# The r and value projections of a time-mix stage as three passes of the rounded format

## What is computed

```python
x_prev = jnp.pad(x, ((0, 0), (1, 0), (0, 0)))[:, :T]
xx = x_prev - x
xs = x[None] + xx[None] * mu[:, None, None, :]
rkv = jnp.einsum('nbtd,nde->nbte', xs[:3], w_rkv)
r, k, v = rkv[0], rkv[1], rkv[2]
w_log = -jax.nn.softplus(-(w0 + jnp.tanh(xw @ w1) @ w2)) - 0.5
a = jax.nn.sigmoid(a0 + (xa @ a1) @ a2)
```

## Time and profile before

| what | value |
|---|---|
| median of 3 runs | 1343.47 us (1342.68 to 1344.71) |
| the profiled execution | 1345.18 us, its span 1343.2 us |
| mean granted clock of PE | 0.997 |
| PE busy | 1310.0 us, 98% of the span |
| DVE, ACT, POOL busy | 936.9, 655.5, 104.6 us |

### The profile page before, as it was taken

The page is one execution under the profiler, slowest core; times in us unless marked ns, Lnnn a source line. Parts: engine busy times, 40 slices in busy tenths (PEclk is TensorE's granted clock), DMA queues, the critical chain, the costliest instruction groups (busy, mean ns, idle before and its releaser), DMA issues.

```text
span 1343.2 us, 23639 instructions
## 1 busy us (share of the span) xinstructions
PE 1310.0 (98%) x9400; PEld 1130.5 (84%) x9400; DVE 936.9 (70%) x1637; ACT 655.5 (49%) x1008; POOL 104.6 (8%) x106
## 2 busy tenths in 40 slices
PE   7999999999999999999999998999999999999999
PEld 7887987888888988888888886888888888888887
DVE  6972456877777765877777697766666786676664
ACT  4532224644445685544445577543434568544431
POOL 0004062000000020000001020000001042000000
PEclk9999999999999999999999999999999999999999
DMA  9532113655543233555551550975531431573610
GB/s 309 162 126 84 47 66 122 224 188 187 187 160 111 93 126 123 201 189 188 188 186 63 188 189 1 340 271 190 186 135 54 165 122 67 220 282 141 235 63 32
DMA packets 113320, 208.51 MB, mean 155 GB/s; under 512 B 3920, under 2 KB 57552, under 8 KB 112720
## 3 DMA queue, kind: packets, MB, share of 16 engines
q1 hardware_dynamic: 113232, 207.28, 44.8%
HBM read 206.21 MB, written 1.05 MB: 154 GB/s over the span
## 4 chain that ended last, share of the span: by engine, by line
PE 87%; DVE 5%; ACT 5%; DMA 1%; issue 1%; POOL 0%; SPq 0%; ACTq 0%; DVEq 0%; POOLq 0%
PE ps L1047 21%; PE ps L994 19%; PE ps L899 11%; PE ps L999 10%; PE ps L1120 2%; PE ps L1089 2%; PE ps L1204 2%; PE ps L1469 2%; PE ps L1377 1%; PE ps L970 1%; ACT Ah L1915 1%; DVE Al L2721 1%; PE ps L1513 1%; DMA ringA<-in_w_k 1%; PE ps L1527 1%
## 5 line engine op out<-in xcount | busy, mean ns | idle before, releaser
L994 PE MATMUL ps<-hTx,Ah 128*128 128x512 f32 x1088 | 270.7, 391 | 0.0
L2728 DVE TENSOR_TENSOR Al<-ringA,Ah 128x2048 fp32r<-128x2048 f32 x74 | 169.3, 2288 | 97.2 <-ACT Ah L1925 97.2
L994 PEld LDWEIGHTS ps<-hTx,Ah 128*128 128x128 f32 x1088 | 199.7, 188 | 38.5
L999 PEld LDWEIGHTS ps<-hTx,Al 128*128 128x128 f32 x1152 | 156.7, 190 | 10.6
L1960 ACT COPY xn<-ps 128x512 f32<-128x512 f32 x72 | 42.3, 587 | 244.1 <-PE ps L999 236.8
L999 PE MATMUL ps<-hTx,Al 128*128 128x256 f32 x1152 | 160.7, 282 | 0.0
L1925 ACT CAST Ah<-ringA 128x2048 fp32r<-128x2048 f32 x76 | 145.7, 1916 | 13.1 <-PE ps L899 10.3
L1934 ACT CAST Bh<-ringB 128x1024 fp32r<-128x1024 f32 (+1 forms) x76 | 107.1, 1410 | 89.5 <-PE ps L1047 89.5
L899 PE MATMUL ps<-Ah,hTx 128*128 128x512 f32 (+1 forms) x576 | 136.6, 388 | 2.8 <-ACT Ah L1915 1.4
L2735 DVE TENSOR_TENSOR Bl<-ringB,Bh 128x1024 fp32r<-128x1024 f32 (+1 forms) x76 | 127.0, 1670 | 10.6 <-ACT Bh L1934 10.2
L1047 PE MATMUL ps<-Bh,hidh 128*128 128x512 f32 x416 | 129.9, 392 | 1.1 <-issue 1.1
(11 more groups left out here) (449 smaller groups left out, 2053.8 us busy)
## 6 DMA issues: line engine op xcount, KB each, us to landing
ringA<-in_ffn_w_in SPq DMA_DIRECT2D x44, 1024.0 KB, 7.5
ringA<-in_mlp_w SPq DMA_DIRECT2D x32, 1024.0 KB, 7.6
ringB<-in_mlp_w SPq DMA_DIRECT2D x32, 1024.0 KB, 6.9
ringB<-in_ffn_w_out SPq DMA_DIRECT2D x44, 512.0 KB, 4.2
ringA<-in_diff_w_in SPq DMA_DIRECT2D x12, 1024.0 KB, 6.3
ringA<-in_dsa_w_in SPq DMA_DIRECT2D x8, 1024.0 KB, 6.2
ringA<-in_w_r SPq DMA_DIRECT2D x4, 1024.0 KB, 8.1
ringA<-in_w_v SPq DMA_DIRECT2D x4, 1024.0 KB, 7.0
```

Of the source, the lines that this page charges most:

```text
L994: mm(o.rearrange("p (i t) -> p i t", i=2), w_hi, hTx[:, :, k * T:(k + 1) * T], start=(k == 0), stop=False)
L999: last = mm(o[:, T:2 * T], Al[:, half, k * T + j * P:k * T + j * P + P], hTh[:, k, :], start=False, stop=(k == KT - 1))
L2728: V.tensor_tensor(a_split(w, Al, half), a_half(w, (a_at[w] + par) % 2, half), a_split(w, Ah, half).bitcast(F32), ALU.subtract).then_inc(al ...
```

## The change

The r and value projections are done in the rounded format too. Each r job becomes 48 matmuls of 128x256 (two halves, three passes, eight steps). Each value job takes a whole 128-token tile and 512 columns: 24 matmuls of 128x512. ACT casts the four r weight quarters, the four value weight halves and the two inputs; the low parts of all of the r side and of value halves 0, 2 and 3 are made by POOL, those of the value input and of value half 1 by DVE. Low parts of weights are written over the weights in `ringA`. The rounded copies lie in buffers that are free at the time. Since some of them lie where a5 is written, a5 now comes after the other two products on DVE and waits for the third r job. The first two value jobs stand one after the other, ahead of `block_rows(0)`. ACT's copy of a value job is split into four copies of 64 partitions each, which stack the heads. New semaphores `rp` and `vp` count high and low parts.

```diff
@@ -460,6 +462,21 @@
+
+        rxh, rxl = over("rxh", "rows", 1024, [P, KT, T]), over("rxl", "ringB", 4096, [P, KT, T])
+        rwh = [over("rwh%d" % i, "arena", a, [P, 2048]) for i, a in enumerate((10240, 18432, 16384))]
+        rwh.append(rwh[0])
+
+        def r_unit(ap, s):
+            return by_k(ap[:, (a_at["w_r"] + s // 2) % 2, :])[:, :, 256 * (s % 2):256 * (s % 2) + 256]
+
+        vxh, vxl = over("vxh", "xn", 0, [P, KT, T]), over("vxl", "ringB", 0, [P, KT, T])
+        vwh = [over("vwh%d" % i, base, at, [P, 2048])
+               for i, (base, at) in enumerate((("arena", 12288), ("rows", 1024),
+                                               ("ringB", 4096), ("ringB", 6144)))]
+
+        def v_half(ap, i):
+            return ap[:, (a_at["w_v"] + i // 2) % 2, 2048 * (i % 2):2048 * (i % 2) + 2048]
         btk = R[2].rearrange("p (j c) -> p j c", j=2)
         eN = kT_
...
@@ -1077,17 +1094,21 @@
                     second(NCH[w] - 1, 1, last_one=True)
-            def feature_job(a0, j0, s, xi):
-
-                a, j = a0 + s // 2, j0 + s
-                if s % 2 == 0:
-                    wait_a(a)
-                b = job_bank(j)
+            def rate_job(s):
+
+                b = job_bank(J["r"][0] + s)
                 for q in range(2):
-                    for k in range(KT):
-                        o = k * 512 + (2 * (s % 2) + q) * P
-                        last = mm(ps[:, b, q * T:(q + 1) * T], ringA[:, a % 2, o:o + P],
-                                  xi[:, k, :], start=(k == 0), stop=(k == KT - 1))
+                    o = slice(q * P, q * P + P)
+                    for i, (w, v, rdy) in enumerate(((by_k(rwh[s][:, :]), rxh, rp["wh"]),
+                                                     (r_unit(ringAl, s), rxh, rp["wl"]),
+                                                     (by_k(rwh[s][:, :]), rxl, None))):
+                        if rdy is not None:
+                            pe.wait_ge(rdy, s + 1)
+                        if i != 1:
+                            pe.wait_ge(rp["xl" if i else "xh"], 1)
+                        for k in range(KT):
+                            last = mm(ps[:, b, q * T:(q + 1) * T], w[:, k, o], v[:, k, :],
+                                      start=(i == 0 and k == 0), stop=(i == 2 and k == KT - 1))
                 last.then_inc(job_rdy, 1)
             def bonus_part(b, p, c, i):
@@ -1096,30 +1117,29 @@
                 return mm(ps[head_rows(i), b, o:o + 1], fm(hflat)[:, p, c * CH:c * CH + CH],
                           con[:, s_:s_ + 1], start=True, stop=True)
-            def value_job(a, j, t, with_bonus=False):
-
-                if t == 0:
-                    wait_a(a)
+            def value_job(slot, j, t, with_bonus=False):
+
                 if with_bonus:
                     pe.wait_ge(wk["rkp"], 1)
                     b2 = job_bank(J["bonus"][0])
                 b = job_bank(j + t)
-                xi = fm(MIXES[5][1])
-                for c2 in range(2):
-                    c = 2 * t + c2
+                for n, (x_, low) in enumerate(((vxh, False), (vxl, False), (vxh, True))):
+                    if n < 2:
+                        pe.wait_ge(vp["xl" if n else "xh"], 1)
                     for k in range(KT):
-                        w = ringA[:, a % 2, k * 512:(k + 1) * 512].rearrange(
-                            "p (q i n) -> p q i n", q=4, i=2)
-                        if with_bonus:
+                        i = 2 * slot + k // 4
+                        w = v_half(ringAl, i) if low else vwh[i][:, :]
+                        if k % 4 == 0 and n != 1:
+                            pe.wait_ge(vp["wl" if low else "wh"], i + 1)
+                        if with_bonus and n < 2:
                             for q in range(2):
-                                for i in range(2):
-                                    ins = bonus_part(b2, k, 2 * c2 + q, i)
-                            if c2 and k == KT - 1:
+                                for h in range(2):
+                                    ins = bonus_part(b2, k, 2 * n + q, h)
+                            if n and k == KT - 1:
                                 ins.then_inc(job_rdy, 1)
-                        for i in range(2):
-                            last = mm(ps[head_rows(i), b, c2 * 256:c2 * 256 + 256],
-                                      xi[:, k, c * CH:c * CH + CH], w[:, :, i, :],
-                                      start=(k == 0), stop=(k == KT - 1))
+                        last = mm(ps[:, b, :], x_[:, k, t * P:(t + 1) * P],
+                                  w[:, (k % 4) * 512:(k % 4) * 512 + 512],
+                                  start=(n == 0 and k == 0), stop=(low and k == KT - 1))
                 last.then_inc(job_rdy, 1)
             def key_sums():
...
@@ -1257,22 +1277,20 @@
                                   lT[i * LORA:(i + 1) * LORA, 0:T], start=True, stop=True)
                         if q:
                             last.then_inc(done, 1)
-            pe.wait_ge(xs_rdy, 10)
             for s in range(4):
-                feature_job(a_at["w_r"], J["r"][0], s, fm(MIXES[4][1]))
+                rate_job(s)
                 if s == 0:
                     key_sums()
                 if s == 1:
                     key_factors()
             for half in range(2):
                 block_products(half)
-            pe.wait_ge(xs_rdy, 12)
-            value_job(a_at["w_v"], J["v"][0], 0)
+            for t in range(NT):
+                value_job(0, J["v"][0], t)
             block_rows(0)
-            value_job(a_at["w_v"], J["v"][0], 1)
-            value_job(a_at["w_v"] + 1, J["v2"][0], 0, with_bonus=True)
+            value_job(1, J["v2"][0], 0, with_bonus=True)
             block_rows(1)
-            value_job(a_at["w_v"] + 1, J["v2"][0], 1)
+            value_job(1, J["v2"][0], 1)
             j = J["bk"][0]
...
@@ -2032,15 +2050,26 @@
                 o = slice(4 * half, 4 * half + 4)
                 act.wait_ge(xs_rdy, half + 1)
                 nc.scalar.copy(kxh[:, o, :], fm(MIXES[3][1])[:, o, :]).then_inc(kp["xh"], 1)
+            def r_round(s, free, n):
+
+                a = a_at["w_r"] + s // 2
+                act.wait_ge(a_loaded[a % 2], 32 * (a // 2 + 1))
+                act.wait_ge(free, n)
+                nc.scalar.copy(by_k(rwh[s][:, :]), r_unit(ringA, s)).then_inc(rp["wh"], 1)
+
             for s in range(2):
                 k_round(2 + s)
                 feature_copies(J["k"][0], kT_, [s])
+            r_round(0, kp["wl"], 3)
             feature_copies(J["k"][0], kT_, [2, 3])
+            act.wait_ge(xs_rdy, 10)
+            nc.scalar.copy(rxh[:, :, :], fm(MIXES[4][1])).then_inc(rp["xh"], 1)
             act.wait_ge(wk["ang"], 1)
             A_(cs2[:, :, :, :], cs2[:, :, :, :], ACT.Sin).then_inc(wk["cs"], 1)
             j = J["lora"][0]
             job(j, lambda p: A_(lT[0:LORA, 0:T], p[0:LORA, 0:T], ACT.Tanh),
                 lambda p: nc.scalar.copy(lT[LORA:2 * LORA, 0:T], p[LORA:2 * LORA, 0:T]))
+            r_round(1, job_rdy, J["k"][0] + 4)
             job(j + 1, lambda p: A_(sigg[:, 0:T], p[:, 0:T], ACT.Sigmoid),
                 lambda p: A_(sigg[:, T:T + CH], p[:, T:T + CH], ACT.Sigmoid))
             j = J["wz"][0]
...
@@ -2055,6 +2084,7 @@
                               bias=col("a0", 2 * s + q))
                 last.then_inc(wk["azo"], 1)
+            r_round(2, job_rdy, J["lora"][0] + 2)
             act.wait_ge(wk["ksum"], 1)
             act.wait_ge(wk["clean"], 1)
             A_(kinv, ps[:, 0, 0:CH], ACT.Sqrt).then_inc(wk["kroot"], 1)
@@ -2063,9 +2093,19 @@
                 job(J["r"][0] + s, lambda p: nc.scalar.copy(rT[:, 512 * s:512 * s + 512], p))
             def v_copy(j, half, t):
-                o = vtok[:, t * D:t * D + D].rearrange("p (c n) -> p c n", c=2)[
-                    :, :, half * 256:half * 256 + 256]
-                job(j + t, lambda p: nc.scalar.copy(o, p.rearrange("p (c n) -> p c n", c=2)))
+                o = 256 * half
+                job(j + t, *[lambda p, c2=c2, i=i: nc.scalar.copy(
+                    chunk(vtok, 2 * t + c2)[head_rows(i), o:o + 256].rearrange("p (q n) -> p q n", q=4),
+                    p[head_rows(c2), :].rearrange("p (q i n) -> p q i n", q=4, i=2)[:, :, i, :])
+                    for c2 in range(2) for i in range(2)])
+
+            def v_round(i, free=None, n=1):
+
+                a = a_at["w_v"] + i // 2
+                act.wait_ge(a_loaded[a % 2], 32 * (a // 2 + 1))
+                if free is not None:
+                    act.wait_ge(free, n)
+                nc.scalar.copy(vwh[i][:, :], v_half(ringA, i)).then_inc(vp["wh"], 1)
             def even_blocks(half):
                 act.wait_ge(wk["nsn"], half + 1)
@@ -2088,20 +2128,28 @@
                                    ).then_inc(wk["nev"], 1)
             r_copy(0)
+            r_round(3, job_rdy, J["r"][0] + 1)
             act.wait_ge(wk["lc"], 1)
```

(45 more changed lines are left out.)

2 lines of the change are left out of this document (added).

## The result

| | before | changed |
|---|---|---|
| median, same chip, 4 runs each | 1344.09 us | 1370.79 us |
| ratio, 95% interval | | 1.0199, 1.0187 to 1.0211 |
| span of the profiled execution | 1343.2 us | 1369.1 us |
| granted clock, mean over the span | 0.997 | 0.984 |

A forecast was written before the change was run, and what follows sets the result against it. PE was taken to bound the kernel nearly everywhere, DVE second in this stage. Block products 20.5 us late, less 6.5 us from value jobs, net +14.0, plus 1.3 for the clock, on 1343.5: 1358.8 us, range 1348 to 1366.

The forecast's parts named there:

- The exclusion: Before the block products, each of six POOL subtractions takes 4.57 us from DVE wherever DVE isn't idle; kinv 20.4 us late.
- six stretches: DVE instructions before 107 us, each lengthened beside a POOL subtraction: four r halves, rxl and the first value half.
- the third: POOL's subtraction for r half 1, placed in the squares of the keys; DVE's scaling of zs 11.3 us later.
- The sixth subtraction: Value half 0, before the block products: operands at 107.2, PE idle 4.6 us, block products 20.5 us late.
- The clock: Behind PE's wait before the block products, a 3 us stretch at the lower clock level, priced at 1.3 us.
- The value jobs: After the block products: each value job 5.44 us instead of 7.06, giving back 6.5 us in four.
- The bonus matmuls are the same in number and stay between others: In the value jobs: the bonus matmuls unchanged by the change, with no cost added for them in the sum.
- The solve late: Second half of the stage: the 6 us of cover before the scan gone, up to 1366 us; chance 0.05.
- The cover holds: Rival: POOL's operations run beside DVE without delaying it, block products 4.4 us earlier, 1332.6 us; chance 0.13.
- part of it: Rival: the exclusion covers only about half of each POOL operation, 1344 us, 1338 to 1350; chance 0.07.
- scans that let POOL pass: Edge of the forecast: r halves 2 and 3 hide under 4.9 of the 5.16 us of scans, 1353.9 us.
- a DVE that doesn't yield: Edge of the forecast: within runs of instructions without waits, low parts come late; scan 5 us later still, 1364 us.

The follow-up runs named there:

- e7: Changed kernel, each GpSimd subtraction replaced by a one-column write (those low parts left out), bonus between float32 matmuls of the first block_rows: 1345.9 us, ratio 1.0008.
- e8: Kernel before with only the r part of the change, its five low parts on GpSimd; values and bonus as before: 1362.4 us, ratio 1.0131.
- e10: Kernel of e1 with all eight GpSimd subtractions moved to VectorE: 1347.1 us, ratio 1.0019.
- e1: Changed kernel with the 64 bonus matmuls as one block ahead of the third value job: 1362.2 us, ratio 1.0131.
- e12: Changed kernel with the bonus in four blocks of 16, ahead of the first block_rows and each third value job pass: 1361.7 us, ratio 1.0133.
- e4: Kernel before with only the values rounded, their low parts on VectorE, bonus as one block ahead of the third value job: 1340.1 us, ratio 0.9963.
- e9: Kernel of e4 with the bonus in four blocks of 16, ahead of the first block_rows and each third value job pass: 1337.9 us, ratio 0.9957.
- e5: Kernel of e4 with the bonus back between the full-width matmuls of the third value job: 1348.9 us, ratio 1.0039.
- e6: Kernel of e4 with at most five bonus matmuls behind each float32 matmul of the first block_rows: 1349.5 us, ratio 1.0042.
- e11: Kernel before, no rounded format added, its bonus as one block ahead of the third value job: 1346.7 us, ratio 1.0014.
- e2: Changed kernel with each of POOL's eight subtractions replaced by two memsets, those low parts zero: 1356.9 us in a single execution.
- e3: Kernel of e2 with the bonus also as one block ahead of the third value job: 1345.8 us in a single execution.

## Why the prediction was right in direction and wrong in size

**The exclusion: right, a little too dear.** All six stretches are there, the scans among them (8.68 us for two subtractions: the scans don't let POOL pass); the third came one group later than in the sum, in the mix for the values and not in the squares of the keys. Each operation took 4.21 to 4.38 us out of DVE's time, where I took the whole 4.57: before the reciprocal 4.38 + 4.21 + 4.28 + 8.68 = 21.55 in place of 22.9 us. With the idle time of 2.41 absorbed, and the stage starting about 1.0 us earlier in the profiled execution (the clock was at 1.00 from 20 to 24 us, where it was down before), kinv was late by 17.9 us, forecast 20.4. The rule that I carried over was also too narrow: it named two inputs on both sides, and the operation held for 4.39 us had one. e7, e8 and e10 show the cause from three sides: without the subtractions the delay is gone, with r's five alone it is whole, and on VectorE they cost half.

**The sixth subtraction: on the path in the forecast, nearly all covered on the chip.** I had PE wait 4.6 us before the block products, at 107.2. They started at 104.62 after 0.83 us of idle time. In both it is the operands from DVE that set the start; they came 2.6 us before the forecast, 1.0 by the earlier start and 1.6 by the cheaper exclusion (25.8 us in place of 27.4 for all six). How PE filled the time until then is the next point.

**The clock: the right effect at the wrong wait, and for nothing.** I put one dip behind the wait for the block products and priced it at 1.3 us. None came there. The long wait was that for the key factors, 12.29 us, and behind it the clock stayed at 0.50 until about 94 us: the key factors took 3.69 us in place of 2.01, and the three groups of r behind them started 1.88, 1.70 and 1.12 us apart in place of 0.95: 3.5 us in all. At full clock PE would have been done with r 3.5 us sooner and would have waited as much longer for the operands. So the dip took the place of a wait and cost nothing on the path. e8 shows the other side. It has no sixth subtraction and no wait before the block products, and counted from the start of the w_z products they come only 0.9 us sooner (47.9 us in place of 48.8), since PE is then what is late.

**The value jobs: right but for a stall.** From the block products to the end of the second value job I had 3.9 + 2 x 5.44 = 14.8 us; it took 16.9 (104.62 to 121.49), of which 1.66 us is one stall of PE at 109.5 for which the profile shows no releaser. It stands in the middle of the first pass, next to the program's wait for the second value half; but that cast had ended at 108.22, 2.9 us before PE went on. The stall appears in e1 and e12 as well and not in e4 and e9; its cause is open.

**The step that failed:** "The bonus matmuls are the same in number and stay between others", priced at nothing. The third value job was to take 5.44 us plus the 3.5 us that the bonus costs in the old one: 8.9. It took 20.7, 11.8 more. With this term the sum is 1358.8 + 11.8 = 1370.6, against 1370.79, and that it comes so near is luck: up to the scan the other terms are off by -2.6 (block products), -1.3 (the clock) and +2.1 us (the first two value jobs), so that the scan starts 9.8 us over the forecast, 0.8 us is added behind it, and the other 1.4 lie between a difference of spans (25.9) and one of medians (27.3).

By its rows the 11.8 us have two halves. At full clock one step of eight bonus records and one rounded matmul takes 0.76 us (125.55 to 126.31), so sixteen steps and the eight matmuls of the last pass would take 14.0 us: 5.1 us for the alternation. The lower clock adds the other 6.7. e5 shows the term without any wait (+8.8 us against the block, +11.0 against four blocks), and e12 takes it out of the change with all the waits left in (-9.1 on the medians, -10.8 on the spans); so the waits have no part in it.

What stood against the assumption was in reach: the earlier trace rows show a job of 64 records of 128x256 (32 float32 matmuls, two records each), and the change leaves 24 in its place. In each of the 16 steps that carry bonus matmuls one record of 0.23 us was to stand, where four of 0.11 each had stood. I counted the bonus and not what stands between it. That this brings the clock down, no row of before showed.

**The solve late:** didn't happen. The solve's products were stretched (1.20 and 4.63 us at 123.90 and 125.14, for 0.41 before), but it ended near 138.7, and the scan, itself 25 us late, found its blocks in time.

**The rivals.** "The cover holds" forecast 1332.6 with the block products 4.4 us early: e7, without subtractions, gives them 5 us early, so that part of its working was right and its premise wrong. Nothing is left of "part of it", of scans that let POOL pass, or of a DVE that doesn't yield: POOL's subtractions took 4.53 to 5.30 us each beside a busy DVE.

**Which part of the change is good.** The values alone, their low parts on VectorE: 5.8 us faster than before with the bonus well placed (e9, by the ratio 0.9957; its median is 7.3 us under that of before). The r part alone: 18.4 us slower on GpSimd, and at best some 3.6 us faster if its low parts were free (e7 against e6).

## What to carry to other kernels

Work given to an idle engine isn't free if that engine and a busy one exclude each other: here a subtraction of some 4.6 us on GpSimd cost VectorE 4.3 us each time, and the 2.29 us on VectorE itself were the cheaper place (e10). Before a format with fewer, wider matmuls is put into a job that carries other small matmuls, count what will stand between the small ones afterwards, and look at the granted clock of the job, not only at PE's busy share, which was 100% here at half speed. When small and wide work must share a stretch, try blocks: the order alone was worth 11 us.

## What the runs showed of the hardware

- **One-column matmuls bring the clock down while PE is busy.** With 64 of them in one block (4.2 to 5.2 us), or eight records between single rounded matmuls, or ten records behind every two of float32, the granted clock went from 1.00 to 0.50 within the run or just behind it, with no idle time in PE's records (e1, e4, e5, e6, e11). With blocks of 1.1 us between passes of 2.03 us (e9, e12), or eight records per two float32 matmuls (four records) of 128x256 (before, e8), it stayed at 1.00. The Trainium skill, "TensorE: Matmul & The Clock Gate", section "HAM oscillation — how this bites in real kernels", ties such losses to gaps in which PE is idle. The waits below agree with it; in these jobs there was no such gap.
- **Alternation costs at full clock too.** Eight bonus records take 0.26 us in a block (1.03 us for 32, e9) and add 0.53 us between rounded matmuls of 128x512 (0.76 less 0.23), but only 0.23 between float32 ones of 128x256 (10.7 less 7.1 us over 16 steps). What it is that costs here, wasn't tried.
- **A MEMSET of 128x2048 on POOL (1.8 us)** held up a pair of TENSOR_SCALAR of 128x256 (2.66 and 3.64 us for 0.61) and didn't touch scans (5.16 us).
- **A wait of 4.5 to 5 us was enough** for the clock to be at 0.50 when PE went on (e2, e3, e10: key factors 3.69 us in place of 2.01). The dip behind it was as dear as the one behind 12 us: 3.8 us in e2 against 3.5.
